# Gate tables inside the first expert, two expert blocks sent ahead, and no barrier behind the experts

## What is computed

```python
def ec_moe(h, w_r, w1, w3, w2):
    B, n, D = h.shape
    cap = max(1, EC_CAPACITY * n // N_EXPERTS)
    aff = jax.nn.softmax((h @ w_r).astype(jnp.float32), axis=-1)
    gate, idx = lax.top_k(jnp.swapaxes(aff, 1, 2), cap)
    xin = jax.vmap(lambda hb, ib: hb[ib])(h, idx)
    hid = jax.nn.silu(jnp.einsum('becd,edf->becf', xin, w1)) * jnp.einsum('becd,edf->becf', xin, w3)
    ye = jnp.einsum('becf,efd->becd', hid, w2) * gate[..., None].astype(h.dtype)
    return jax.vmap(lambda yb, ib: jnp.zeros((n, D), h.dtype).at[ib.reshape(-1)].add(yb.reshape(-1, D)))(ye, idx)
...
        h2 = modulate(rmsnorm(x, g_norm2[i]), sh2, sc2)
        x = x + gt2 * ec_moe(h2, w_router[i], w_e1[i], w_e3[i], w_e2[i])
        if not last:
            h2c = modulate(rmsnorm(xc, g_norm2[i]), sh2c, sc2c)
            xc = xc + gt2c * ec_moe(h2c, w_router[i], w_e1[i], w_e3[i], w_e2[i])
    return rmsnorm(x, g_final)
```

## Time and profile before

| | us |
|---|---|
| median of 3 runs | 2837.45 |
| the runs | 2834.03, 2837.45, 2837.53 |
| the profiled execution | 2834.02 |
| its span | 2832.2 |
| TensorE (PE) busy in it | 2541.3 |
| VectorE (DVE), ScalarE (ACT), GpSimd (POOL) busy | 1045.9, 882.3, 426.8 |

### The profile page before, as it was taken

How to read it: one execution, slowest core, us unless ns; L and a number is a source line. 1 busy time by engine, 2 the same in 40 slices (tenths; PEclk the granted TensorE clock), 3 DMA queues, 4 the chain that set the end, 5 groups by cost and what they waited for, 6 DMA issues and landing times. The chain is left out here.

```text
span 2832.2 us, 36664 instructions
## 1 busy us (share of the span) xinstructions
PE 2541.3 (90%) x15228; PEld 1808.8 (64%) x15228; DVE 1045.9 (37%) x1526; ACT 882.3 (31%) x1395; POOL 426.8 (15%) x217
## 2 busy tenths in 40 slices
PE   7999989999999999899998788887998998887877
PEld 7888878899998778688852222224776983222223
DVE  4548632336764534444440011114455652000001
ACT  4465543344443343422231000002334441000001
POOL 0430017680000231000310000000132011000000
PEclk9999999999999999899999999999999999999998
DMA  5434327764543221322279999996212449999995
GB/s 215 164 135 163 107 73 298 298 231 170 180 165 134 75 71 45 149 104 90 102 316 427 428 427 428 427 428 253 104 60 86 164 179 373 428 428 428 428 427 247
DMA packets 66573, 669.50 MB, mean 236 GB/s; under 512 B 7264, under 2 KB 8432, under 8 KB 10736
## 3 DMA queue, kind: packets, MB, share of 16 engines
q1 hardware_dynamic: 63936, 654.62, 58.2%
q0 software_dynamic: 2208, 11.56, 1.2%
q10 hardware_dynamic: 272, 1.05, 0.1%
HBM read 666.13 MB, written 1.06 MB: 236 GB/s over the span
## 5 line engine op out<-in xcount | busy, mean ns | idle before, releaser
L593 PE MATMUL ps<-A,piece_hi 128*128 128x256 f32 (+1 forms) x1952 | 617.1, 316 | 20.6 <-ACTq L479 7.2
L594 PE MATMUL ps<-A,piece_hi 128*128 128x256 f32 (+1 forms) x1952 | 604.8, 310 | 0.0
L595 PE MATMUL ps<-A,ring_lo 128*128 128x256 f32 (+1 forms) x1952 | 604.4, 310 | 0.0
L492 ACT ACTIVATE piece_hi<-ring 128x1024 fp32r<-128x1024 f32 x378 | 393.3, 1054 | 210.5 <-DVEq L631 104.8
L2499 PE MATMUL ps<-ring,WK 128*64 128x512 f32 x1680 | 381.6, 598 | 81.2 <-DMA ring<-in_blocks 63.3
L593 PEld LDWEIGHTS ps<-A,piece_hi 128*128 128x128 f32 x1952 | 376.7, 193 | 59.9 <-issue 24.8
L503 POOL TENSOR_TENSOR ring_lo<-ring,piece_hi 128x1024 fp32r<-128x1024 f32 x123 | 312.4, 2551 | 680.1 <-ACT piece_hi L492 623.8
L501 DVE TENSOR_TENSOR ring_lo<-ring,piece_hi 128x1024 fp32r<-128x1024 f32 x255 | 317.3, 1249 | 255.1 <-ACT piece_hi L492 254.6
L595 PEld LDWEIGHTS ps<-A,ring_lo 128*128 128x128 f32 x1952 | 377.1, 193 | 18.1
L594 PEld LDWEIGHTS ps<-A,piece_hi 128*128 128x128 f32 x1952 | 377.2, 193 | 17.7
L2499 PEld LDWEIGHTS ps<-ring,WK 128*64 128x64 f32 x1680 | 113.0, 136 | 328.5 <-issue 193.9
(11 more groups left out here) (277 smaller groups left out, 2991.5 us busy)
## 6 DMA issues: line engine op xcount, KB each, us to landing
ring<-in_stream SPq DMA_DIRECT2D x237, 1024.0 KB, 5.0
ring<-in_blocks SPq DMA_DIRECT2D x104, 2048.0 KB, 20.7
WK<-in_blocks SPq DMA_DIRECT2D x36, 2048.0 KB, 20.7
hi_place<-in_blocks SPq DMA_DIRECT2D x34, 2048.0 KB, 20.7
A_place<-in_blocks SPq DMA_DIRECT2D x15, 2048.0 KB, 25.6
WK<-in_na_bias POOLq DMA_DIRECT2D x2, 2048.0 KB, 7.9
WK<-cum_scratch POOLq DMA_DIRECT2D x1, 2048.0 KB, 11.0
ring<-in_blocks SPq DMA_DIRECT2D x2, 1024.0 KB, 18.7
```

The lines of the kernel that those rows point to most:

```text
L492: nc.scalar.activation(piece_hi[:, no % 4, :], ring[:, slot, at:at + PIECE], ACT.Copy).then_inc(hi_done[no % 4], 1)
L593: nc.tensor.matmul(out_, l[0], r[0], start=first, stop=False)
L594: nc.tensor.matmul(out_, l[0], r[1], start=False, stop=False)
L595: return nc.tensor.matmul(out_, l[1], r[0], start=False, stop=last)
```

## The change

Three edits.

1. **Gate tables in the first expert.** `route_*` no longer make PH and GT. VectorE makes PH at the start of `experts_dve`; TensorE turns it in expert 0, behind w3's blocks, into four banks that expert 0 doesn't use; ScalarE copies it to GT behind HIDT; TensorE's expert 1 waits for the copies. HID, SG and HIDT move from WK to the free half of A_place, since PH now lives into expert 0.
2. **Two blocks ahead.** SP sends layer 0's blocks 0 and 1 (`hi`, `far`) ahead of the last ten loads of the stream, slots 14 to 23 of the modulation.
3. **No barrier behind the experts.** The scatter waits for the saved rows and the last additions instead. The splits of the next pieces stand behind the scatter and the squares. In the last layer the barriers up to the end go too: VectorE multiplies each finished chunk by the gain `g_final` (GAINED), TensorE turns four chunks ahead of the norm's sums and four behind, and the norm's factor is applied to rows while they are copied out of PSUM, half the rows on ScalarE, half on VectorE. Two DMAs issued by SP write them.

```diff
-        HID, SG = wk(18432, 2, 512), wk(18432 + 1024, 512)
-        HIDT = wk(18432 + 1536, 4, P)
+        hidden = A_place[:, 0].rearrange("p k t -> p (k t)")
+        HID, SG = hidden[:, 0:1024].rearrange("p (a w) -> p a w", a=2), hidden[:, 1024:1536]
+        HIDT = hidden[:, 1536:2048].rearrange("p (c s) -> p c s", c=4)
...
+        GATE_BANKS = (2, 3, 5, 7)
+        def gates_scaled_dve(dve, st):
...
+            for m in range(2 * st):
+                ins = nc.vector.tensor_tensor(ph[:, m], f32(one_hot[:, m]), AFF[:, m, :].unsqueeze(2).to_broadcast([P, EXPERTS, CAP]),
+                                              ALU.mult)
+            ins.then_inc(onehot, 1)
+        def gates_turn_pe(pe, cur, st):
+            pe.wait_ge(onehot, 2 * cur.base("route"))
+            for i in range(2 * st):
+                for g_ in range(2):
+                    for m in range(2):
+                        last = nc.tensor.transpose(ps[:, GATE_BANKS[i], g_ * T + m * P:g_ * T + m * P + P],
+                                                   PH[:, 2 * (i // 2) + m, (2 * (i % 2) + g_) * P:(2 * (i % 2) + g_ + 1) * P], ident)
+                last.then_inc(gate_turned, 1)
...
         def experts_pe(pe, cur, st, layer):
+                if e == 1:
+                    pe.wait_ge(gate_copied, gates_turned(layer + 1))
...
                 last.then_inc(moe_g, 1)
+                if e == 0:
+                    gates_turn_pe(pe, cur, st)
                 pe.wait_ge(moe_hid, n + 1)
...
         def scatter_pe(pe, cur, st):
+            pe.wait_ge(moe_saved[0], cur.base("moe"))
+            pe.wait_ge(moe_saved[1], cur.base("moe"))
             for c in range(DC):
+                if c == 2:
+                    pe.wait_ge(moe_added, cur.base("back") + 24)
...
+        def final_dve(dve, cur):
+            g0 = cur.g
+            def behind(c):
+                if c > 0:
+                    gain_dve(dve, c - 1, g0 + c - 1, cur)
+            scatter_dve(dve, cur, 1, LAYERS - 1, behind)
+            gain_dve(dve, DC - 1, cur.g - 1, cur)
...
+            for h, at in enumerate((g + 1, g + 4)):
+                dve.wait_ge(bank_full[cur.bank(at)], cur.bank_use(1, at))
+                nc.vector.tensor_scalar(OUT[:, 1, h * 512:(h + 1) * 512], ps[:, cur.bank(at), :], nvar[:, 1:2], None,
+                                        ALU.mult).then_inc(rows_dve, 1)
...
-            run(R, EXPERTS_AT[0] // 2)
-            blocks(0)
+            run(R, EXPERTS_AT[0] // 2 - 10)
+            first_blocks(0, [0, 1])
+            run(EXPERTS_AT[0] // 2 - 10, EXPERTS_AT[0] // 2)
+            first_blocks(0, [5, 2, 3, 4])
+            blocks(0, 6)
...
+            sp.wait_ge(rows_act, 2)
+            sp.dma_start(rows[:, 0, :], OUT[:, 0, :]).then_inc(stored, 16)
+            sp.wait_ge(rows_dve, 2)
+            sp.dma_start(rows[:, 1, :], OUT[:, 1, :]).then_inc(stored, 16)
+            sp.wait_ge(stored, 32)
...
                 experts_pe(pe, cur, n // T, layer)
-                barrier(pe, cur)
                 scatter_pe(pe, cur, n // T)
-                norm_sums_pe(pe, cur, SQ_BACK, n)
-                barrier(pe, cur)
-            norm_spread_pe(pe, cur, T)
-            barrier(pe, cur)
-            turn_out_pe(pe, cur)
-            barrier(pe, cur)
+                if layer == LAYERS - 1:
+                    turn_out_pe(pe, cur, 0)
+                    norm_sums_pe(pe, cur, SQ_BACK, n)
+                    turn_out_pe(pe, cur, 1)
+                else:
+                    norm_sums_pe(pe, cur, SQ_BACK, n)
+                    barrier(pe, cur)
```

More of the change, by code:

```diff
@@ L2629, in scatter_pe, with scatter_dve @@
             cur.add("back", 24)
-        def scatter_dve(dve, cur, st, layer):
+        def scatter_dve(dve, cur, st, layer, behind=lambda c: None):
+            dve.wait_ge(moe_added, cur.base("back") + 24)
             for c in range(DC):
@@ new lines, in final_act @@
+        def final_act(act, cur, steps):
+            for c in range(DC):
+                skip_banks(cur, 1)
+                square_act(act, cur, SQ_BACK, T, c, cur.g - 1)
+            table(steps, ACT.Sqrt)
+            g = cur.g
+            skip_banks(cur, 5)
+            act.wait_ge(bank_free[cur.bank(g + 2)], cur.bank_use(1, g + 2))
+            nc.scalar.activation(nvar[:, 0:TT], nvar[:, 0:TT], ACT.Sqrt).then_inc(norm_sd, 1)
+            act.wait_ge(rstd_ready, NORMS)
+            for h, at in enumerate((g, g + 3)):
+                act.wait_ge(bank_full[cur.bank(at)], cur.bank_use(1, at))
+                nc.scalar.activation(OUT[:, 0, h * 512:(h + 1) * 512], ps[:, cur.bank(at), :], ACT.Copy,
+                                     scale=nvar[:, 0:1]).then_inc(rows_act, 1)
@@ L2721, in load_block, with first_blocks @@
                     sp.dma_start(block_place(name), words).then_inc(block_landed[name], 16)
-            def blocks(layer):
-                first = [0, 1, 5, 2, 3, 4] if layer == 0 else [0, 1, 2, 3, 4, 6, 7, 5]
-                for b in first:
+            def first_blocks(layer, order):
+                for b in order:
                     name = BLOCK_AT[layer][b]
@@ L2744, in _ @@
             run(EXPERTS_AT[0] // 2 + R, EXPERTS_AT[1] // 2)
-            blocks(1)
+            first_blocks(1, [0, 1, 2, 3, 4, 6, 7, 5])
+            blocks(1, 8)
+            rows = out.rearrange("a (m p) d -> p (a m) d", p=P)
+            sp.wait_ge(rows_act, 2)
[3 more added lines that the diff above has]
+            sp.wait_ge(stored, 32)
         @block.tensor
@@ L2933, in _ @@
                 experts_act(act, cur, n // T, layer)
-                barrier(act, cur)
-                for c in range(DC):
-                    skip_banks(cur, 1)
-                    square_act(act, cur, SQ_BACK, n, c, cur.g - 1)
-                table(steps, ACT.Sqrt)
-                barrier(act, cur)
-            main_norm_act(act, cur, steps, T, split=False)
-            barrier(act, cur)
-            turn_out_act(act, cur)
-            barrier(act, cur)
+                if layer == LAYERS - 1:
+                    final_act(act, cur, steps)
+                else:
+                    for c in range(DC):
+                        skip_banks(cur, 1)
+                        square_act(act, cur, SQ_BACK, n, c, cur.g - 1)
+                    split_ahead(act, cur)
+                    table(steps, ACT.Sqrt)
+                    barrier(act, cur)
             ended.append((cur.stage, cur.p, cur.g))
-            act.dma_start(out.rearrange("a (m p) d -> p (a m) d", p=P), OUT).then_inc(stored, 16)
-            act.wait_ge(stored, 16)
         @block.vector
```

89 lines of the change are left out of this document (47 added, 42 removed).

## The result

The changed kernel takes 2805.97 us (median of 4 runs, 2804.20 to 2807.87), the kernel before 2837.49 in the same comparison (4 runs, 2834.03 to 2838.48). The ratio is 0.9891, with a 95% interval of 0.9877 to 0.9905: 31.5 us less. The forecast was 2811.4, so 26.0 us less, with a range of 2803 to 2819: direction and range hold, the size is 5.5 us short.

The account below looks back on a forecast made before the run. Transfers were taken to bound the experts, TensorE and its hand-overs everywhere else. Terms of 7.5, 6.6, 2.9 and 9.0 sum to 26.0 us, taken from the median of 2837.45 for 2811.4 us, range 2803 to 2819.

Parts of the forecast that it names:

- term B: Passage from layer 0 to 1: scatter starts without TensorE's idle, splits come behind it; 6.6 us gained, ends 8.1 and 5.0.
- Term A: Layer 0: blocks 0 and 1 sent ahead and experts begun earlier; 7.5 us gained, ends 9.8 and 2.4.
- Rival 1: Layer 0's start: TensorE paces it and the dry queue doesn't refill, gain there only 2.4 us, total 2816.5; 12%.
- rival 4: Layer 0's route: modulation slots land late, experts 5 us later, gain there turns to -2.6 us, total 2821.5; 4%.
- rival 5: Experts: TensorE's clock falls to 1.2 GHz, costing 15 us per expert, slower overall, 2871 at four experts; 3%.
- squares end at about 1952.2: Passage from layer 0 to 1: step placing the squares' end, from the table load's 1960.34 less 8.1.
- Term C: Layer 1's experts: start earlier with no PH and GT ahead of them; 2.9 us gained, ends 3.1 and 2.0.
- Term D: Tail: norm's factor applied last as a scale of rows, four barriers gone; 9.0 us gained, ends 11.5 and 7.
- its square at 2814.4: Tail: step placing the square of the last product, ready at 2814.0, ahead of the root's table at 2815.9.
- Rival 3: Tail: each gain held for a GpSimd addition and 1.2 GHz throughout, tail gains 6.5 us, total 2813.9; 12%.
- the 1.2 GHz end of the range: Tail: TensorE's eight transposes take 1.8 us at 1.2 GHz, not 1.0 at 2.4 GHz; its end between 2817.0 and 2819.0.
- Rival 2: Layer 0 gains 9.8 us and tail 11.5, 30.8 in all, total 2806.6; gains never meet GpSimd, 2.4 GHz; 13%.

Follow-up runs that it names:

- e12: The changed kernel run again without any edit, for a second trace and more runs: 2802.97 us.
- e1: Changed kernel with SP's order undone, layer 0's first two blocks again behind the ten stream loads: 2810.9 us.
- e3: Kernel before with SP's order alone changed, two blocks ahead of the ten loads: 2832.2 us.
- e4: Kernel before with the gate tables alone moved into the first expert: 2831.4 us.
- e7: Changed kernel with only the barrier put back between layer 0's last expert and the scatter, splits still behind the squares: 2806.9 us.
- e8: Changed kernel with only the three splits put back ahead of the scatter's additions and squares, no barrier: 2813.5 us.
- e9: Kernel of e5 with 18 idle products filling TensorE's gap ahead of the barrier: 2814.2 us.
- e10: Changed kernel with one output write of 1 MB instead of two of 0.5 MB: 2806.0 us.
- e2: Changed kernel with the gate tables (PH, its transposes and GT) made in the route again: 2811.4 us.
- e5: Changed kernel with the passage from layer 0 to 1 undone, splits and a barrier again ahead of the scatter: 2813.4 us.
- e6: Changed kernel with the tail undone: split, barriers, norm's products, turn and one write as before: 2812.3 us.
- e11: Changed kernel with GpSimd doing one of its four additions of squares in the last layer, TensorE summing the other chunks: 2805.1 us.

## Why the prediction was right, and where its sizes were off

By stage, without the 3.9 us up to R, the two traces differ by 31.4 us: 7.2 (R to G0), 8.2, 1.7, 2.8 and 11.5. The medians say 31.5. Of the 5.5 us by which the forecast fell short, 1.6 lie in term B, 1.7 in a stage for which it had no term, and 2.5 in the tail; A and C together came out 0.4 below it.

**Term A, 7.5 forecast, 7.2 measured** (e12: 6.9). Block issues at R, experts 2.05 behind the last XIN copy instead of about 2.0, transposes in expert 0 1.97, full queue from block 6 on (DMA share 0.99 to 1.03 from 60 us behind R). The dry time ahead of it was some 1.4 us, not 2 to 3. Block 11 came 1.2 later than worked out (1517.1 with the 3.9 taken off), block 6 landing 0.5 late and the last engine of each block a little more; the forecast had taken 0.6 off for that. The mechanism behind it, transfers bound and places short, is what e1, e3 and e4 show. Rival 1 (2.4 us) falls: the gain stood until G0. So does rival 4: the 32 products on slots 12 to 15 started at 1446.28, exactly 3.89 later than in the earlier trace rows, as the whole stage; nobody waited for a slot. The experts' stretch 1500:1600 shows 1.00 at 85% busy, so rival 5 falls too.

**Term B, 6.6 forecast, 8.2 measured.** The step that failed is "squares end at about 1952.2": it took the 10.3 us from the scatter's start to the end of the squares from a stretch that ran partly at 1.2 GHz (8.72 for the 32 products). At 2.4 GHz it is 8.6 (1938.47 to 1947.1). The rest came as worked out: three splits 2.93, table and first use 1.5, the barrier 0.6 behind. e7 and e8 say what in B pays: the splits' place, 7.6 us, and hardly the barrier, 1.6. The title's "no barrier behind the experts" names the smaller part. In e9 the clock could not be had for itself. The last 1.6 us are won because in the new order the low clock falls on waits and idle products instead of the scatter or the sums: the granted clock is 1.00 from the scatter's start to 1949.6 and 0.50 from 1950.6. A further 1.7 us appear between N and R1, in code that no edit touches, and the forecast had no term for them. TensorE's busy time there says that the clock has a hand in it, and e10 has the new passage and 366.0 all the same. It doesn't settle all of it: e3 has the busy time of the changed kernel (338.5) and 365.6.

**Term C, 2.9 forecast, 2.8 measured** between R1 and G1. The first freed place is issued 32.8 behind R1 instead of 35.8 (2349.54 and 2365.67) and lands after 7.6 like then. e2 and e3, with the tables in the route, have 476.1 and 476.6, most others 472.4 to 473.2; e4, e5 and e10, with 474.3 to 474.7, began the stage at the low clock.

**Term D, 9.0 forecast, 11.5 measured against that trace, 8.8 to 9.5 against the old tail of e6, e3 and e4.** That 9.0 fits the latter is luck: the sum subtracted from the slow tail of 26.7 and made the new one 17.7 long; it is 15.2. Its steps, from G1: last gain 7.6 instead of 8.4, since GpSimd held the gains for 0.5 and not 1.2, and a pair of addition and gain took 0.65 without the hold (e11) against the 0.69 summed, though a gain by itself took 0.34 and not 0.29. The factor 9.5 instead of 11.1: the step "its square at 2814.4" let ScalarE's last square wait for the last gain, but a square waits for the addition alone, and the table load began 0.1 before the last gain's end. Rows 10.9 instead of 13.0, TensorE being through before the factor, at 2.4 GHz. The write from its issue to the end 4.0, not 4.6. To their landing the first of the two took 2.6, the second 3.6 behind it, and the single megabyte of e10 4.0. The rule of the Trainium skill ("SBUF — State Buffer", The DMA setup-cost knee) gives estimates of 3.2 for a half and 4.4 for the whole, more than the first half and the whole took. Rival 3 (new waits, 6.5) and the 1.2 GHz end of the range fall.

Rival 2 (gains 30.8) was the nearest in number: its D of 11.5 came true with TensorE at 2.4 GHz, though the gains did meet GpSimd; its A of 9.8 did not.

In the tail each hold is only 0.09 to 0.16 us. The rows show why. GpSimd's four additions, one row of 3.33 above, start at 2792.81, 2793.80, 2794.60 and 2795.41 and take 0.91, 0.72, 0.73 and 0.73. The four long gains end at 2793.87, 2794.67, 2795.49 and 2796.29, each 0.15 to 0.16 behind the end of one of them, as the held operation in the earlier trace rows did (0.15). The gains start every 0.81 us (2794.99, 2795.80), the last additions as well, so each gain comes only 0.34 before an addition ends, and the two run in step. The Trainium skill ("SBUF — State Buffer", Who interferes with whom) has an instruction held at the shared port for the whole of the other's; these ends agree. The hold, though, costs only the difference of the two paces (0.81 less 0.65), for as long as GpSimd is at work, not a full instruction each. The forecast had no way of seeing that, for the earlier trace rows show one hold in isolation. Its 0.78 for an addition was read from a merged row: before, one took 0.73 on average, with short gaps between.

## What to carry to other kernels

Where transfers bound a stage, look for both what fills the queue early and what frees places early: here one alone gave 0.2 us, the other 3.2, both 7.2. When an operation that waits for a late load stands ahead of the path in an engine's queue, moving it behind can be worth more than the barrier that made it visible (here 7.6 against 1.6 us). Before a duration from a profile goes into a sum, read which clock it ran at, and compare executions stage by stage: the same old tail was 24.0 or 26.7 us long, and the same code up to the route differed by 8.4 us between two profiles of one program.

## What was not expected of the hardware

Products of nothing that bridged an idle of 8 us kept the scatter at 2.4 GHz (7.14 against 8.93 in e5) and moved the time at 1.2 GHz to the sums behind it (4.63 against 2.84), so the sum of both stayed at 11.77. And VectorE and GpSimd, of which one was held until the other's operation ended, fell into step at 0.81 us, so that the holds cost 0.5 us over eight gains instead of a GpSimd addition each.
